# Down projection of a SwiGLU block: eight of eleven row blocks as four pairs of seven products

## The reference, cut to what matters

```python
xs = xs + g1x[:, None, :] * out_x
xs = xs + g2x[:, None, :] * _swiglu(_modulate(_rmsnorm(xs, norm2_g[l]), sh2x, sc2x), w_ff1[l], w_ff3[l], w_ff2[l])
return _rmsnorm(xs, final_g)

def _swiglu(h, w1, w3, w2):
    a = jnp.einsum('bnd,df->bnf', h, w1)
    g = jnp.einsum('bnd,df->bnf', h, w3)
    return jnp.einsum('bnf,fd->bnd', jax.nn.silu(a) * g, w2)
```

## Time and profile before

| | |
|---|---|
| Median of 3 runs | 1835.89 us (1835.03 to 1836.02) |
| Profiled execution, its own time | 1837.14 us |
| Its span in the trace | 1835.5 us |
| Granted TensorE clock, mean over the span | 0.988 |
| TensorE, VectorE, ScalarE, GpSimd busy | 1778.0, 1090.8, 597.5, 166.3 us |

### The profile page before, as it was taken

The page is one execution under the profiler, slowest core; times in us unless marked ns, Lnnn a source line. Parts: engine busy times, 40 slices in busy tenths (PEclk is TensorE's granted clock), DMA queues, the critical chain, the costliest instruction groups (busy, mean ns, idle before and its releaser), DMA issues.

```text
span 1835.5 us, 23349 instructions
## 1 busy us (share of the span) xinstructions
PE 1778.0 (97%) x8636; PEld 1487.3 (81%) x8636; DVE 1090.8 (59%) x1706; ACT 597.5 (33%) x935; POOL 166.3 (9%) x202
## 2 busy tenths in 40 slices
PE   6899999999999999999999999999999999999997
PEld 3697988979797888788888888888888888778886
DVE  4587636465556466555432445775565656676667
ACT  6533231423222313444310213533343333312112
POOL 1002020200112000111200000000000001232210
PEclk9999999999999899999999999999999999999999
DMA  7211111202068022423733243123222232632212
GB/s 303 67 48 35 59 47 44 71 23 70 12 217 311 8 84 69 160 98 106 271 99 92 91 161 126 35 75 109 69 91 69 83 100 69 246 132 91 91 46 92
DMA packets 99730, 186.65 MB, mean 102 GB/s; under 512 B 5674, under 2 KB 74426, under 8 KB 95314
## 3 DMA queue, kind: packets, MB, share of 16 engines
q1 hardware_dynamic: 83906, 130.11, 21.0%
q0 software_dynamic: 15760, 55.68, 8.7%
HBM read 149.04 MB, written 36.73 MB: 101 GB/s over the span
## 4 chain that ended last, share of the span: by engine, by line
PE 83%; DVE 8%; DMA 4%; issue 3%; ACT 1%; DVEq 0%; SPq 0%; POOL 0%; POOLq 0%; ACTq 0%
PE PD L2065 23%; PE PD L2483 10%; PE PM L2483 10%; PE PD L2503 6%; PE PM L2503 6%; PE PD L2398 5%; PE PM L2346 4%; PE PD L2346 4%; PE PD L2081 3%; DMA ada<-in_w_ada 3%; PE PM L2417 1%; PE PD L2417 1%; PE PD L2150 1%; DVE kT L1432 1%; PE PM L2323 1%
## 5 line engine op out<-in xcount | busy, mean ns | idle before, releaser
L2065 PE MATMUL PD<-R_hi,whi 128*128 128x512 f32 x480 | 150.3, 395 | 0.0
L2065 PE MATMUL PD<-R_lo,whi 128*128 128x512 f32 x480 | 149.1, 392 | 0.0
L2065 PE MATMUL PD<-R_hi,wlo 128*128 128x512 f32 x480 | 148.9, 392 | 0.0
L841 POOL TENSOR_TENSOR w_raw<-w_raw,g2B 128x2048 f32<-128x2048 f32 x11 | 52.0, 4730 | 638.6 <-DMA w_raw<-in_w_ff 638.6
L2065 PEld LDWEIGHTS PD<-R_hi,wlo 128*128 128x128 f32 x480 | 90.7, 189 | 19.2
L2065 PEld LDWEIGHTS PD<-R_lo,whi 128*128 128x128 f32 x480 | 90.7, 189 | 19.1
L2065 PEld LDWEIGHTS PD<-R_hi,whi 128*128 128x128 f32 x480 | 89.7, 189 | 18.6 <-issue 0.7
L1858 DVE TENSOR_TENSOR ws_lo<-S,ws_hi 128x512 fp32r<-128x512 f32 x76 | 56.3, 742 | 77.2 <-ACT ws_hi L1210 77.2
L868 ACT ACTIVATE whi<-raw 128x1024 fp32r<-128x1024 f32 x56 | 56.1, 1049 | 126.7 <-PE PD L2065 124.0
L2081 PE MATMUL PD<-whi,R_hi 128*128 128x256 f32 x256 | 72.9, 285 | 0.8 <-ACT vaug L934 0.8
L2081 PE MATMUL PD<-wlo,R_hi 128*128 128x256 f32 x256 | 72.6, 283 | 0.0
(11 more groups left out here) (479 smaller groups left out, 4665.4 us busy)
## 6 DMA issues: line engine op xcount, KB each, us to landing
rawF<-in_w_ff SPq DMA_DIRECT2D x44, 512.0 KB, 5.2
ada<-in_w_ada POOLq DMA_DIRECT2D x32, 512.0 KB, 6.2
raw<-in_w_in SPq DMA_DIRECT2D x30, 512.0 KB, 5.4
f_dram<-Fo SPq DMA_DIRECT2D x11, 1024.0 KB, 4.8
w_raw<-in_w_ff SPq DMA_DIRECT2D x11, 1024.0 KB, 5.0
f_raw<-f_dram SPq DMA_DIRECT2D x11, 1024.0 KB, 6.9
ada_raw<-in_w_ada SPq DMA_DIRECT2D x8, 1024.0 KB, 19.4
rawG<-in_w_in SPq DMA_DIRECT2D x16, 512.0 KB, 5.6
```

The source lines that it names most:

```text
L841: nc.gpsimd.tensor_tensor(w2_raw[par], w2_raw[par], g2B[:, :].unsqueeze(1).to_broadcast([P, 2, D]), ALU.mult)\
L2065: i = mm(dst[:, e * HALF:e * HALF + width], wk[:, k, :], part, start=(k == 0 and step == 0), stop=(k == KT - 1 and step == 2))
```

## The change

Row blocks 1 to 8 are taken in four pairs. A pair is a product of 1024 x 512 by 512 x 1024. Its operands are cut in two each way: `a[m][k]` of `f` and `b[k][n]` of `w2`, each 128x1024 in SBUF. Seven products of 512 x 256 by 256 x 512 take the place of the eight, 24 matmuls each (`down_product`).

- Sums of operands are on GpSimd. `first_down_sums` has four, for products 1 and 2; `second_down_sums` has four, for products 3, 4 and 6. They use two buffers for the left and two for the right operands (`dS`, `dT`), so each waits until the lo part of the product that last read its buffer is made.
- The hi and lo parts of each product's left and right operand (128x1024) are made on ScalarE and VectorE and are put into one of four places, four products ahead.
- Products go in turn to the two sets of four PSUM banks. Products 2, 3 and 4 keep adding into what products 0 and 1 left there. After each product VectorE adds the whole set (128x2048) into one quarter of `xs2` (`down_add`). What product 4 leaves is wanted in two quarters. In the first three pairs ScalarE copies it to `u3` and GpSimd adds that to the second quarter (`add_u3`); in the last pair VectorE adds twice.
- The loads of the first pair and of half the residual tiles come later: `w2` blocks 1 and 2 after the sixth product of the last up block, then `f` blocks 1 and 2 and tiles 4 to 7 after its seventh. Before, all followed its fifth or fourth.
- Row blocks 0, 9 and 10 are computed as before.

The core of the diff (waits and helpers that only count semaphores are left out):

```diff
+PAIRS = (NFB - 3) // 2
+DOWN = PAIRS * PRODUCTS
+D_OPENS = (True, True, False, False, False, True, True)
+D_CLOSES = (False, False, False, True, True, True, True)
+D_INTO = ((0, 0), (1, 1), (0, 1), (0, 1), (1, 0), (0, 0), (1, 0))
+U3_AT = 4
+S_AT = {1: 1, 2: 2, 3: 3, 4: 4}
+T_AT = {1: 1, 2: 2, 4: 3, 6: 4}
+LEFTS_UP, SUMS_UP, T_UP, COPIES_UP = GB * PRODUCTS, (GB + 2 * (NFB - 1)) * 4, 2 * 4, (GB + 2 * (NFB - 1)) * 4
...
+        def down_place(i, part):
+            R, at = ((R_hi, 4), (R_lo, 0), (R_lo, 4), (R_hi, 0))[i % 4]
+            return R[:, at + part, :].rearrange("p (k n) -> p k n", k=2)
...
+        def down_left(i):
+            g, n = divmod(i, PRODUCTS)
+            f = f_pair[g % 2]
+            if n in S_AT:
+                return dS[1 - n % 2][:, :, :]
+            return down_part(f, *{0: (0, 0), 5: (1, 0), 6: (1, 1)}[n])
+        def down_right(i):
+            g, n = divmod(i, PRODUCTS)
+            w = w_pair[g % 2]
+            if n in T_AT:
+                return dT[{1: 0, 2: 1, 4: 0, 6: 1}[n]][:, :, :]
+            return down_part(w, *{0: (0, 0), 3: (1, 1), 5: (1, 0)}[n])
...
+            sp.wait_ge(product, LAST + 6 + LEFTS_UP)
+            sp.wait_ge(w2_in[0], 16)
+            load_w2(1)
+            load_w2(2)
+            sp.wait_ge(product, LAST + 7 + LEFTS_UP)
+            sp.wait_ge(f_in[0], 16)
+            load_f(1)
+            load_f(2)
             load_xs(4, LT)
...
+            for g in range(1, PAIRS + 1):
+                if g >= 2:
+                    sp.wait_ge(down_ready, down_right_lo((g - 2) * PRODUCTS + 6))
+                for k in range(2):
+                    sp.wait_ge(w2_in[k], down_loaded(2 * g - 1 + k))
+                    load_w2(2 * g + 1 + k)
+                for k in range(2):
+                    sp.wait_ge(f_in[k], down_loaded(2 * g - 1 + k))
+                    load_f(2 * g + 1 + k)
...
+            def first_down_sums(g):
+                a, b = parts_of(g)
+                i = g * PRODUCTS
+                for k in range(2):
+                    pool.wait_ge(f_in[k], down_loaded(2 * g + 1 + k))
+                if g == 0:
+                    pool.wait_ge(product, LAST + 6 + LEFTS_UP)
+                else:
+                    pool.wait_ge(down_ready, down_left_lo(i - PRODUCTS + 3))
+                nc.gpsimd.tensor_tensor(dS[0][:, :, :], a[1][0], a[1][1], ALU.add).then_inc(s_made, 1)
+                pool.wait_ge(w2_scaled, 2 * g + 3)
+                pool.wait_ge(down_ready, 1 if g == 0 else down_right_lo(i - PRODUCTS + 4))
+                nc.gpsimd.tensor_tensor(dT[0][:, :, :], b[0][1], b[0][0], ALU.subtract).then_inc(t_made, 1)
+                pool.wait_ge(s_made, SUMS_UP + 4 * g + 1)
+                if g > 0:
+                    pool.wait_ge(down_ready, down_left_lo(i - PRODUCTS + 4))
+                nc.gpsimd.tensor_tensor(dS[1][:, :, :], dS[0][:, :, :], a[0][0], ALU.subtract).then_inc(s_made, 1)
+                pool.wait_ge(t_made, T_UP + 4 * g + 1)
+                if g > 0:
+                    pool.wait_ge(down_ready, down_right_lo(i - PRODUCTS + 6))
+                nc.gpsimd.tensor_tensor(dT[1][:, :, :], b[1][1], dT[0][:, :, :], ALU.subtract).then_inc(t_made, 1)
+            def second_down_sums(g):
+                a, b = parts_of(g)
+                i = g * PRODUCTS
+                pool.wait_ge(s_made, SUMS_UP + 4 * g + 2)
+                pool.wait_ge(down_ready, down_left_lo(i + 1))
+                nc.gpsimd.tensor_tensor(dS[0][:, :, :], a[0][1], dS[1][:, :, :], ALU.subtract).then_inc(s_made, 1)
+                pool.wait_ge(t_made, T_UP + 4 * g + 2)
+                pool.wait_ge(down_ready, down_right_lo(i + 1))
+                nc.gpsimd.tensor_tensor(dT[0][:, :, :], b[1][1], b[0][1], ALU.subtract).then_inc(t_made, 1)
+                pool.wait_ge(s_made, SUMS_UP + 4 * g + 3)
+                pool.wait_ge(down_ready, down_left_lo(i + 2))
+                nc.gpsimd.tensor_tensor(dS[1][:, :, :], a[0][0], a[1][0], ALU.subtract).then_inc(s_made, 1)
+                pool.wait_ge(down_ready, down_right_lo(i + 2))
+                nc.gpsimd.tensor_tensor(dT[1][:, :, :], b[1][0], dT[1][:, :, :], ALU.subtract).then_inc(t_made, 1)
+            def add_u3(g):
+                i = g * PRODUCTS
+                pool.wait_ge(snapped, COPIES_UP + g + 1)
+                pool.wait_ge(summed, down_added(i + 1))
+                nc.gpsimd.tensor_tensor(down_into(1, 1), u3[:, :, :], down_into(1, 1), ALU.add).then_inc(combined, 1)
...
+            for g in range(PAIRS):
+                second_down_sums(g)
+                scale_w2(2 * g + 3)
+                scale_w2(2 * g + 4)
+                if g < PAIRS - 1:
+                    first_down_sums(g + 1)
+                    add_u3(g)
...
+            def down_operands_hi(i):
+                g, n = divmod(i, PRODUCTS)
+                if i < 3:
+                    act.wait_ge(product, LAST + 5 + LEFTS_UP)
+                else:
+                    act.wait_ge(down_done, down_made(i - 4))
+                if n in S_AT:
+                    act.wait_ge(s_made, SUMS_UP + 4 * g + S_AT[n])
+                else:
+                    act.wait_ge(f_in[n > 0], down_loaded(2 * g + 1 + (n > 0)))
+                nc.scalar.activation(down_place(i, 0), down_left(i), ACT.Copy).then_inc(down_hi_d, 1)
+                if n in T_AT:
+                    act.wait_ge(t_made, T_UP + 4 * g + T_AT[n])
+                else:
+                    act.wait_ge(w2_scaled, 2 * g + (2 if n == 0 else 3))
+                nc.scalar.activation(down_place(i, 2), down_right(i), ACT.Copy).then_inc(down_hi_d, 1)
+            def copy_u3(g):
+                i = g * PRODUCTS + U3_AT
+                act.wait_ge(down_done, down_made(i))
+                act.wait_ge(summed, down_added(i))
+                if g > 0:
+                    act.wait_ge(combined, SUMS_UP + g)
+                nc.scalar.activation(u3[:, :, :], sets[i % 2], ACT.Copy).then_inc(snapped, 1)
...
+            for i in range(4):
+                down_operands_hi(i)
+            for i in range(DOWN):
+                if i % PRODUCTS == U3_AT and i < DOWN - PRODUCTS:
+                    copy_u3(i // PRODUCTS)
+                if i + 4 < DOWN:
+                    down_operands_hi(i + 4)
...
+            def down_operands_lo(i):
+                dve.wait_ge(down_hi_d, down_left_lo(i))
+                v.tensor_tensor(down_place(i, 1), down_left(i), down_place(i, 0).bitcast(F32), ALU.subtract)\
+                    .then_inc(down_ready, 1)
...
+            def down_add(i):
+                g, n = divmod(i, PRODUCTS)
+                dve.wait_ge(down_done, down_made(i))
+                dve.wait_ge(summed, down_added(i - 1) if i else 4 + LT)
+                if n == 1 and g > 0:
+                    dve.wait_ge(combined, SUMS_UP + g)
+                at = down_into(*D_INTO[n])
+                v.tensor_tensor(at, sets[i % 2], at, ALU.add).then_inc(summed, 1)
...
+                accumulate(1, 4, t)
+                if t in (4, 6, 7):
+                    down_operands_lo({4: 0, 6: 1, 7: 2}[t])
+            down_operands_lo(3)
+            for i in range(DOWN):
+                down_add(i)
+                if i + 4 < DOWN:
+                    down_operands_lo(i + 4)
...
-            with pe.Fori(0, (NFB - 3) // 2) as i:
-                down_group(i * 2 + 1, 1)
-                down_group(i * 2 + 2, 0)
...
+            def down_product(i):
+                n = i % PRODUCTS
+                pe.wait_ge(down_ready, down_right_lo(i))
+                pe.wait_ge(summed, down_added(i - 2) if i >= 2 else 4 + (LT - 2 + 2 * i))
+                if i >= 2 and (i - 2) % PRODUCTS == U3_AT and i < DOWN - PRODUCTS:
+                    pe.wait_ge(snapped, COPIES_UP + i // PRODUCTS + 1)
+                left, right = [down_place(i, p) for p in range(2)], [down_place(i, 2 + p) for p in range(2)]
+                for t in range(4):
+                    at = slice(t * P, (t + 1) * P)
+                    for k in range(2):
+                        for step, (lt, rt) in enumerate(((left[0], right[0]), (left[0], right[1]),
+                                                         (left[1], right[0]))):
+                            last = mm(held[i % 2][t], lt[:, k, at], rt[:, k, :],
+                                      start=(D_OPENS[n] and k == 0 and step == 0),
+                                      stop=(D_CLOSES[n] and k == 1 and step == 2), skip_group_check=True)
+                last.then_inc(down_done, 1)
```

More of the change, by code:

```diff
@@ L283, in build @@
                 w2_raw0 = sb("w2_raw0", [P, 2, D], stack=s7)
+            with ExitStack() as s7:
+                dT = [sb(f"dT{n}", [P, 2, HALF], stack=s7) for n in range(2)]
             rawF = [sb("rawF0", [P, KT, CW], stack=sF)]
@@ L291, in build @@
                 f_hi0 = sb("f_hi0", [P, 2, NLAT], F32R, s7)
+                with ExitStack() as s8:
+                    u3 = sb("u3", [P, 4, HALF], stack=s8)
```

(39 more changed lines are left out.)

178 lines of the change are left out of this document (100 added, 78 removed).

## The result

The changed kernel takes 1864.74 us (median of 4 runs, 1863.59 to 1865.78); the kernel before, timed beside it, takes 1835.95 (4 runs, 1835.03 to 1839.35). The ratio is 1.0153, 95% interval 1.0136 to 1.0171: slower by 28.8 us. The profiled execution took 1864.43 us for a span of 1862.7.

A forecast was written before the change was run, and what follows sets the result against it. Turns at the SBUF port shared by GpSimd and VectorE bound it: 48.4 plus 4.3 makes 52.7 us a pair. Row block 9 starts 33.4 later, so 1837.1 + 33.4 = 1870.5, predicted 1870, range 1850 to 1900.

The forecast's parts named there:

- The deciding step: the port: In a pair, GpSimd instructions and VectorE's two-SBUF-input lo's take turns without overlap: 48.4 us against TensorE's 38.1.
- sum of 48.4 us for the port: Per pair, GpSimd's sums, scalings and `u3` addition (32.6 us) plus VectorE's lo's (15.8); adds need no turn.
- walk of turns: Instruction-by-instruction order of VectorE and GpSimd through a pair, longer waiter first: 52.7 us, 4.3 above 48.4.
- the rival's 1811: Rival for the pairs: GpSimd's sums run beside VectorE's lo's, TensorE bounds, forecast 1809 us; chance 0.08.
- the first rival's turning point: The result turns faster once a pair's port time falls under 43.5 us, needing a third of lo's free.
- A: VectorE's 128x2048 add of a product's PSUM banks into `xs2`: needs no turn, stays at 2.2 to 2.4 us.
- clusters: Expected in the profile: down-projection lo's at about 1.2 us, and at 1.2 plus the rest of a sum or scaling.
- busy 70 to 75% of a pair: Expected in the profile: TensorE's busy share in a pair of about 53 us, waiting on VectorE's adds.
- The clock: TensorE's clock falls after gaps of 3.7 and 6.1 us in a pair, 2.5 us lost each; hidden, otherwise 20 us.
- No turns: Rival: sums on GpSimd overlap VectorE's lo's, TensorE bounds, row block 9 is 26.7 us earlier, 1809 us; chance 0.08.
- The clock stays low: Rival: matmuls at 0.43 us make TensorE the bound over 28 products, 1946 us; part beyond 1900, chance 0.09.
- Gains and losses cancel: Rival: first and last pair pack far better than walked, time 1832 to 1840 us; chance 0.03.

The follow-up runs named there:

- the kernel with 38.7: Against the changed kernel, all 32 operand sums moved from GpSimd to VectorE, scalings and `u3` left on GpSimd: 1880.24 us.
- the new split: Against the changed kernel: `dT` sums and `u3`'s addition on VectorE, scalings halved, first add earlier; GpSimd free 1851.66 us, held to start beside adds 1826.08.

## Why the prediction was right

**The deciding step: the port.** Right. The prediction's sum of 48.4 us for the port and its walk of turns gave a pair of 52.7; it is 51.5. Memsets in place of the sums freed their lo's and nothing else, and without any reads of GpSimd's the time fell to the rival's 1811. The walk was the right tool, and the sum of 48.4 beside it only a bound: with a port total of 38.7 the time rose to 1880. "This is the sum that decides" was too strong, then, and so was the first rival's turning point, a port time under 43.5: the kernel with 38.7 is the slowest. The reason the walk gives and the total doesn't is that the one engine whose list is long enough to matter is VectorE, and only GpSimd work that falls beside its adds is free.

**The sizes, to the start of row block 9.** Predicted 1813.8, measured 1807.9, so 5.9 too late:

- 2.2 from row block 0, which started at 1577.07 in the profile after and at 1579.27 in that of before. No step of the change.
- 2.0 in the first pair: its fifth add ended 67.4 us after row block 0's start, not 69.4. The first add came 16.2 us after that block's end, not 18 (17.7 by the walk).
- 2.4 in the two whole pairs (1.2 each). I had priced a sum at 2.35, as for one with nothing beside it. In turns with lo's a sum and a lo come every 3.35 us (1655.57, 1658.93, 1662.27), so the sum costs 2.2; seven of the eight sums of a pair meet a lo, which makes about 1 of the 1.2.
- 0.7 the other way in the last pair, 60.4 instead of 59.7. One add waits 1.2 us for TensorE there, which the walk did not have.

With that, 1870 against 1864.7. Row block 0's start moves by up to 7.5 us from run to run, so a single trace to start from allows no better than that: that the forecast came within 0.3% is in part luck, the pair of 51.5 for 52.7 is not.

**The signs.** A stayed untouched (2.28, with 2.2 from start to start). The lo's lie in clusters, but in three: 1.2, about 3.4 and 4.8 to 5.6, by which GpSimd instruction they met. The sums take 2.4 to 3.4, product matmuls number 672. TensorE was to be busy 70 to 75% of a pair and is shown at 83%: I had divided 38.1 by the pair and left out that products after the gaps run at the lower clock and count as busy.

**The clock.** Right in place and size, and nearly all hidden. The walk had gaps of 3.7 and 6.1 us in a pair with 2.5 lost after each; in the pair shown they are 3.42 and 5.23, the products after them take 8.32 and 8.09, that is 2.7 and 2.5 longer than 5.6, and of all 28 adds one waits for TensorE, 1.2 us in the last pair: for a product that took 7.79 behind a gap of 5.35. That it is otherwise off the path was argued from the walk, and leaving a third of the matmuls out showed it. One reading was loose: the prediction called both of its gaps as long as the one of 4.12 us after which the clock had fallen, and 3.7 is not; the clock fell behind both.

**The rivals.** "No turns" needed lo's that stay at 1.2 beside a sum; none did. "The clock stays low" needed it over the whole stage; it was at 0.87 to 0.94 of full speed there. "Gains and losses cancel" would have needed 28 us less in packing; packing alone gave 25.6 in the new split, whose work is another, and needed an order and waits that the change does not have.
